# An out-projection in two halves of its rows, and a new order in a differential attention, in a two-block transformer kernel

## The reference

```python
h = rms_norm_2(x, mix_norm_g[layer])
proj = h @ w_in[layer]
da_q, da_k, da_v, sb_q, sb_k, sb_v, c_q, c_kv, k_r = jnp.split(proj, pts, axis=-1)
y_a = diff_attention(da_q, da_k, da_v, ...)        # 4 heads, columns 0 to 511 of y
y_b = stick_breaking(sb_q, sb_k, sb_v, ...)        # 4 heads, columns 512 to 767
y_c = latent_attention(c_q, c_kv, k_r, ...)        # 4 heads, columns 768 to 1023
x = x + jnp.concatenate([y_a, y_b, y_c], axis=-1) @ w_out[layer]
```

## Time and profile before

| | |
|---|---|
| median of three runs | 3553.13 us |
| the profiled execution | 3550.04 us |
| its span | 3548.2 us |
| TensorE matmuls, busy | 3166.5 us, 89% |
| VectorE, busy | 1626.1 us, 46% |
| ScalarE, busy | 1455.8 us, 41% |
| GpSimd, busy | 759.2 us, 21% |
| mean granted TensorE clock | 0.927 |

### The profile page before, as it was taken

One profiled execution on the slowest core, in us unless ns is written; L12 is line 12 of the kernel. 1 busy time (PEld: TensorE's weight loads), 2 busy tenths in 40 slices (PEclk: granted clock), 3 DMA queues, 4 the chain that ended last, 5 costly groups with the idle time before them and its releaser, 6 DMA issues.

```text
span 3548.2 us, 43654 instructions
## 1 busy us (share of the span) xinstructions
PE 3166.5 (89%) x13571; PEld 2479.1 (70%) x13571; DVE 1626.1 (46%) x2425; ACT 1455.8 (41%) x2128; POOL 759.2 (21%) x320
## 2 busy tenths in 40 slices
PE   7999999799997757999968978699998897879998
PEld 5788887588885545888746756488876664658887
DVE  4544544666565437565556344421125535351113
ACT  3333333433344545343344555432334455442323
POOL 1233232000002310000021212144432111214442
PEclk8999999899998878999978989799998898979999
DMA  8322222233331212333221211133332111213332
GB/s 201 96 86 78 66 86 60 76 96 96 94 90 42 74 45 83 93 93 95 65 78 36 55 48 42 30 95 93 92 88 85 48 53 33 60 29 93 94 94 77
DMA packets 486165, 269.41 MB, mean 76 GB/s; under 512 B 9418, under 2 KB 477458, under 8 KB 485620
## 3 DMA queue, kind: packets, MB, share of 16 engines
q1 hardware_dynamic: 479236, 255.85, 25.6%
q10 hardware_dynamic: 6768, 11.62, 1.0%
HBM read 264.12 MB, written 12.21 MB: 78 GB/s over the span
## 4 chain that ended last, share of the span: by engine, by line
issue 54%; PE 29%; POOL 11%; DVE 3%; ACT 2%; DMA 0%; SPq 0%; POOLq 0%; ACTq 0%; DVEq 0%
POOL s_w_lo L625 11%; PE acc L664 8%; PE acc L665 8%; PE acc L670 7%; PE acc L667 1%; PE wide L691 1%; PE misc L938 1%; PE misc L665 0%; PE misc L664 0%; PE misc L670 0%; PE wide L664 0%; DMA s_raw<-attn_w_qkv 0%; SPq L520 0%; DVE s_sc L2022 0%; POOLq L102 0%
## 5 line engine op out<-in xcount | busy, mean ns | idle before, releaser
L625 POOL TENSOR_TENSOR s_w_lo<-s_raw,s_w_hi 128x1024 fp32r<-128x1024 f32 x316 | 759.0, 2402 | 2760.3 <-ACT s_w_hi L1236 2755.2
L664 PE MATMUL acc<-s_h_hi,s_w_hi 128*128 128x512 f32 (+1 forms) x2128 | 873.5, 410 | 119.5 <-POOL s_w_lo L625 44.4
L665 PE MATMUL acc<-s_h_lo,s_w_hi 128*128 128x512 f32 (+1 forms) x2128 | 847.0, 398 | 0.0
L670 PE MATMUL acc<-s_h_hi,s_w_lo 128*128 128x512 f32 (+1 forms) x1862 | 741.3, 398 | 0.0
L664 PEld LDWEIGHTS acc<-s_h_hi,s_w_hi 128*128 128x128 f32 x2128 | 409.1, 192 | 238.2 <-issue 73.0
L1236 ACT ACTIVATE s_w_hi<-s_raw 128x1024 fp32r<-128x1024 f32 x388 | 411.7, 1061 | 387.1 <-DVE s_x L2527 210.9
L665 PEld LDWEIGHTS acc<-s_h_lo,s_w_hi 128*128 128x128 f32 x2128 | 410.5, 193 | 94.9 <-issue 7.1
L670 PEld LDWEIGHTS acc<-s_h_hi,s_w_lo 128*128 128x128 f32 x1862 | 358.6, 193 | 83.9
L664 PE MATMUL acc<-s_hid_hi,s_w_hi 128*128 128x512 f32 x752 | 297.4, 395 | 0.0
L665 PE MATMUL acc<-s_hid_lo,s_w_hi 128*128 128x512 f32 x752 | 297.3, 395 | 0.0
L670 PE MATMUL acc<-s_hid_hi,s_w_lo 128*128 128x512 f32 x658 | 260.0, 395 | 0.0
(11 more groups left out here) (395 smaller groups left out, 4875.3 us busy)
## 6 DMA issues: line engine op xcount, KB each, us to landing
s_raw<-w_ff SPq DMA_DIRECT2D x128, 512.0 KB, 4.0
s_raw<-ffn_w_up SPq DMA_DIRECT2D x96, 512.0 KB, 3.9
s_raw<-attn_w_qkv SPq DMA_DIRECT2D x72, 512.0 KB, 3.6
s_raw<-ffn_w_down SPq DMA_DIRECT2D x48, 512.0 KB, 3.9
s_raw<-w_in SPq DMA_DIRECT2D x44, 512.0 KB, 4.0
s_raw<-lru_w_in SPq DMA_DIRECT2D x16, 512.0 KB, 3.9
s_raw<-w_out SPq DMA_DIRECT2D x16, 512.0 KB, 4.0
s_raw<-attn_w_o SPq DMA_DIRECT2D x8, 512.0 KB, 4.1
```

The costliest lines, as they stand in the source:

```text
L625: pool.tensor_tensor(w_lo_of[w][:], raw_b[s][:], w_hi_of[w][:].bitcast(F32), ALU.subtract).then_inc(sems["unit_ready"], 1)
L664: mm(out, ahi, bhi, start=start, stop=False, **kw)
L665: mm(out, ahi, blo, start=False, stop=False, **kw)
L670: mm(out, alo, bhi, start=False, stop=stop, **kw)
```

## The change

The weights of `w_out` are loaded in another cut: four units of rows 0 to 511 x 256 columns, then four of rows 512 to 1023 x 256 columns. The first four chunks of y, which the differential attention makes, are split at the start of the latent attention into `early_hi` and `early_lo` (memory of the stick-breaking queries and keys, and two free chunks of `h_hi` and `h_lo`). The first half is multiplied inside the latent attention, as 8 tiles of 12 matmuls: tiles 0 to 3 into `misc`, two in the prologue and one in each of heads 0 and 1, tiles 4 to 7 into the two banks, around the softmax of head 3. VectorE adds each onto x. The second half stands where the out-projection stood, with 12 matmuls per tile; tiles 0 and 1 do chunks 4 to 6 before chunk 7 is there. ScalarE's splits of weights go with it: two before the four casts, two in head 2, two in head 3, four in `onto_residual`.

In the latent attention the sum of the query's squares comes before the rotation, and the key's sum goes to a bank of its own, so that ScalarE takes both Ln from different places; the casts of the key come first.

In the differential attention the scores of a head are issued between the chunks of the next query unit, the transposes of its weights before every second chunk of the next value unit, and the key's sum before chunk 3 of that unit, from a second buffer of squares. The sum over a head's output comes behind the value transpose, and its norm before the next head's scores on VectorE. The three units with which stick-breaking begins are issued under head 3, and the norm of that head's output inside `sb_heads`. In the diff some 8 or 12 columns of indentation are cut.

```diff
+early_hi = [t_[:] for t_ in (qh, ql, kh, kl)]
+early_lo = [t_[:, c, :] for t_ in (h_hi, h_lo) for c in (6, 7)]
 by_token = lambda ap: ap.rearrange("p k n -> p (k n)").rearrange("p (t c) -> p t c", t=TT)
...
-    for n in range(KC):
-        unit(wo2[:, :, n * P:(n + 1) * P])
+    for first in (0, KC // 2):
+        for n in range(KC // 2):
+            s = raw_b[count.slot()]
+            part_unit(s[:].rearrange("p k n -> p (k n)").rearrange("p (k n) -> p k n", k=KC // 2),
+                      wo2[:, first:first + KC // 2, n * 2 * P:(n + 1) * 2 * P])
...
+    next_unit = lambda before=None: unit_of(h_hi, h_lo, before=before)
+    def da_scores(k):
+        q, m = divmod(k, 2)
+        w = (q + 1) * P
+        o, r = next_wide(), slice(q * P, w)
+        three(o[:, 0:w], qh[half(m), r], ql[half(m), r], kh[half(m), 0:w], kl[half(m), 0:w],
+              True, True, "wide_full")
+    def da_turn(k):
+        q = k // 2
+        if k % 2 == 0:
+            pe.wait_ge(sems["p_ready"], count("p_ready"))
+            turn4(next_wide(), [sd[:, 0, TRI[q] + j * P:TRI[q] + (j + 1) * P] for j in range(q + 1)], "wide_full")
+    def da_keys_sum(k):
+        if k == 3:
+            head_sum(HALVES, first=1)
+    def da_turn_and_sum(k):
+        da_turn(k)
+        da_keys_sum(k)
+    next_unit(lambda k: pe.wait_ge(sems["h_lo"], count("h_lo")))
+    stats()
+    next_unit()
+    head_sum(HALVES)
+    next_unit(da_keys_sum)
+    turn_v()
     for h in range(HEADS_2):
-        unit_of(h_hi, h_lo, before=(lambda k: pe.wait_ge(sems["h_lo"], count("h_lo"))) if h == 0 else None)
-        if h == 0:
-            stats()
-        unit_of(h_hi, h_lo)
-        head_sum(HALVES)
-        if h:
-            turn_a()
-        unit_of(h_hi, h_lo)
-        head_sum(HALVES)
-        if h:
+        pe.wait_ge(sems["hn_lo"], count("hn_lo", 2))
+        next_unit(da_scores)
+        next_unit()
+        if h < HEADS_2 - 1:
+            head_sum(HALVES)
+            next_unit(da_turn_and_sum)
             weigh_values()
-        turn_v()
-        pe.wait_ge(sems["hn_lo"], count("hn_lo", 2))
-        for q in range(TT):
-            for m in range(2):
-                w = (q + 1) * P
-                o, r = next_wide(), slice(q * P, w)
-                three(o[:, 0:w], qh[half(m), r], ql[half(m), r], kh[half(m), 0:w], kl[half(m), 0:w],
-                      True, True, "wide_full")
-        if h:
+            turn_v()
             head_sum(ONES)
-    turn_a()
-    weigh_values()
-    head_sum(ONES)
+        else:
+            next_unit(da_turn)
+            weigh_values()
...
+        head_sum(ONES, MLA_W, squared="mla_sq")
+        pe.wait_ge(sems["mla_sq"], count("mla_sq"))
+        if past := count("acc_freed", lag=count.banks):
+            pe.wait_ge(sems["acc_freed"], past)
+        mm(bank[count.bank()][0:MLA_W, :], square[0:MLA_W, ONES, 0:MLA_W], sq[0:MLA_W, 1, :], start=True,
+           stop=True).then_inc(sems["acc_full"], 1)
+        count("acc_full")
+        count.outs += 1
...
+    count.units += 2
+    def out_chunks(o, n, chunks, hi, lo, start, stop):
+        w = lambda of, c: flat(of, count.slot())[:, (c % 4) * 2 * P + n % 2 * P:(c % 4) * 2 * P + n % 2 * P + P]
+        for c in chunks:
+            last = stop and c == chunks[-1]
+            mm(o, w(w_hi_b, c), hi[c], start=start and c == chunks[0], stop=False)
+            mm(o, w(w_hi_b, c), lo[c], start=False, stop=False)
+            if last:
+                mm(o, w(w_lo_b, c), hi[c], start=False, stop=True).then_inc(sems[stop], 1)
+                count(stop)
+            else:
+                mm(o, w(w_lo_b, c), hi[c], start=False, stop=False)
+    def early_tile(n, o, sem):
+        if n % 2 == 0:
+            pe.wait_ge(sems["unit_ready"], count("unit_ready"))
+        out_chunks(o, n, range(4), early_hi, early_lo, True, sem)
+        if n % 2:
+            count.units += 1
+    def early_in_misc(n):
+        take_misc("dve")
+        early_tile(n, misc[:], "wo_full")
+    def early_in_bank(n):
+        if past := count("acc_freed", lag=count.banks):
+            pe.wait_ge(sems["acc_freed"], past)
+        early_tile(n, bank[count.bank()][:], "acc_full")
+        count.outs += 1
     mla_values()
     mla_products(0)
+    pe.wait_ge(sems["o_lo"], count("o_lo", 4))
+    early_in_misc(0)
     head_sum(HALVES)
+    early_in_misc(1)
     head_sum(HALVES)
     take_misc("dve")
...
     mla_sums()
-    for h in range(HEADS_2):
-        if h < HEADS_2 - 1:
-            mla_products(h + 1)
+    for h in range(HEADS_2 - 1):
+        mla_products(h + 1)
         mla_scores(h)
         if h:
             mla_weigh(h - 1, TT)
-        if h < HEADS_2 - 1:
-            mla_sums()
+        if h < 2:
+            early_in_misc(2 + h)
+        mla_sums()
         if h == 2:
             head_sum(HALVES)
         mla_turn()
+    mla_scores(HEADS_2 - 1)
+    mla_weigh(HEADS_2 - 2, TT)
+    early_in_bank(4)
+    early_in_bank(5)
+    mla_turn()
+    early_in_bank(6)
     mla_weigh(HEADS_2 - 1, 0)
+    early_in_bank(7)
     head_sum(HALVES)
-    count.units += 2
+    late = ([ys_hi[:, c, :] for c in range(KC)], [ys_lo[:, c, :] for c in range(KC)])
     for n in range(KC):
-        unit_of(ys_hi, ys_lo, before=(lambda k: pe.wait_ge(sems["o_lo"], count("o_lo"))) if n == 0 else None)
+        if n % 2 == 0:
+            pe.wait_ge(sems["unit_ready"], count("unit_ready"))
+        if n == 0:
+            first = [bank[(count.outs + b) % count.banks] for b in range(2)]
+            for b in range(2):
+                pe.wait_ge(sems["acc_freed"], count("acc_freed", lag=count.banks))
+                for c in (4, 5, 6):
+                    if b == 0:
+                        pe.wait_ge(sems["o_lo"], count("o_lo"))
+                    out_chunks(first[b][:], b, [c], *late, c == 4, None)
+            pe.wait_ge(sems["o_lo"], count("o_lo"))
+        if n < 2:
+            out_chunks(first[n][:], n, [7], *late, False, "acc_full")
+        else:
+            if past := count("acc_freed", lag=count.banks):
+                pe.wait_ge(sems["acc_freed"], past)
+            out_chunks(bank[count.bank()][:], n, range(4, KC), *late, True, "acc_full")
+        count.outs += 1
+        if n % 2:
+            count.units += 1
...
+        head_square(tn[:, 1, :], part=1)
         head_rstd(SUB)
         head_hi(qh[:], tn[:, 0, :], SUB ** -0.5)
-        head_square(tn[:, 1, :])
...
+    for c in range(4):
+        fn(early_hi[c], yo[:, c, :], ACT.Copy).then_inc(sems["o_hi"], 1)
+        act.wait_ge(sems["o_hi"], count("o_hi"))
     norm_output(SUB)
     fn(sq[:, 0, :].rearrange("p (n k) -> p n k", n=2), tn[:, :, 0:N_MEM], ACT.Square).then_inc(sems["hn_sq"], 1)
...
     def mla_hi(h):
         head_rstd(MLA_W, MLA_W)
-        head_rstd(MLA_W, MLA_W, dst=sd[0:MLA_W, 1, S:2 * S])
+        rs_k = sd[0:MLA_W, 1, S:2 * S]
+        act.wait_ge(sems["acc_full"], count("acc_full"))
+        fn(rs_k, bank[count.bank()][0:MLA_W, :], ACT.Ln, bias=eps[0:MLA_W, 0:1], scale=1.0 / MLA_W).then_inc(sems["mla_ln"], 1)
+        count("acc_freed")
+        count.outs += 1
+        act.wait_ge(sems["mla_ln"], count("mla_ln"))
+        fn(rs_k, rs_k, ACT.Exp, scale=-0.5).then_inc(sems["hn_rstd"], 1)
+        act.wait_ge(sems["hn_rstd"], count("hn_rstd"))
+        freed()
...
+    nc.vector.memset(bd[0:CHUNK, :, S - CHUNK:S], NEG).then_inc(sems["bd_cut"], 1)
+    dve.wait_ge(sems["bd_cut"], count("bd_cut"))
+    for h in range(HEADS_2):
+        da_scores(h)
+        if h < HEADS_2 - 1:
+            o = output()
+            scaled(tn[:, 0, :], o[:])
+            da_weights()
+            o = output()
+            scaled(tn[:, 1, :], o[:])
+            da_queries()
+            turned_a()
+            da_keys()
+            values()
+            take_output()
+            turned_v()
+            da_output(h)
+        else:
+            sb_lo(0)
+            da_weights()
+            sb_lo(1)
+            turned_a()
+            values()
+            take_output()
...
         count("wide_freed")
+    for c in range(4):
+        dve.wait_ge(sems["o_hi"], count("o_hi"))
+        tt(early_lo[c], yo[:, c, :], early_hi[c].bitcast(F32), ALU.subtract).then_inc(sems["o_lo"], 1)
+        count("o_lo")
+    def early_from_misc(n):
+        dve.wait_ge(sems["wo_full"], count("wo_full"))
+        tt(x[:, n, :], x[:, n, :], misc[:], ALU.add).then_inc(sems["misc_dve"], 1)
+        count("misc_dve")
+    def early_from_bank(n):
+        o = output()
+        tt(x[:, n, :], x[:, n, :], o[:], ALU.add).then_inc(sems["acc_freed"], 1)
+        count("acc_freed")
+    early_from_misc(0)
     head_norm([(yo[:, 5, :], od[:], 0)], "sb_out_g_2")
+    early_from_misc(1)
     keys = tn[:, :, 0:N_MEM]
...
+        dve.wait_ge(sems["hn_rstd"], count("hn_rstd", 2))
+        output()
+        tt(kr[R, :], tn[R, 1, :], rs_k[R, :], ALU.mult).then_inc(sems["acc_freed"], 1)
+        dve.wait_ge(sems["acc_freed"], count("acc_freed"))
```

(28 more changed lines are left out.)

153 lines of the change are left out of this document (76 added, 77 removed).

## The result

| | median, us | runs | range |
|---|---|---|---|
| before | 3552.49 | 4 | 3548.35 to 3557.21 |
| changed | 3619.82 | 4 | 3618.24 to 3623.18 |

The ratio is 1.019, with a 95% interval from 1.0173 to 1.0208. Forecast was 3517, in a range up to 3543. The loss is 67 us, some 34 in each layer. The page of the changed kernel answers to the earlier trace rows: as many matmuls as before, and TensorE busy 93.5 us longer.

A forecast was written before the change was run, and what follows sets the result against it. The prediction took matmuls to bound the whole kernel, but VectorE-ScalarE-TensorE chains its attention stages. Differential -10.6 and latent -7.2 us per layer, twice, gave -35.6: 3514.4 from the profiled 3550.0, 3517 on the median's footing; 8-in-10 range 3485 to 3543.

The forecast's parts named there:

- 8 additions and 8 maxima, 3.9 + 3.9 less overlap: 15.6: Differential head: VectorE's additions and maxima on the scores end 15.6 us after the end of `s_kl`.
- 26.3 us of PE work: Differential head: unit matmuls, scores, sums, transposes and values total 26.3 us, under a chain of 34.5 us.
- First chain: Differential head 0: the key sum runs inside the value unit, so its chain ends earlier, -3.3 us per layer.
- Tail: Differential head 3 to first stick-breaking score: 32.8 us instead of 42.4, -9.6 per layer.
- Moved sum: One sum moves from the differential tail into the stick-breaking stage, where PE has no gap: +0.9 us per layer.
- Latent prologue: Latent attention up to its first scores: net +10 us per layer, bounds +4 and +13.
- late half: Second half of the out-projection: VectorE's work of 25.4 us in 22.4 of matmuls costs 0, at worst +4.
- The collisions: Differential weights: two GpSimd operations of 2.5 us fall on the four multiply-adds, 2.0 us more per head.
- rival 1: Collisions on the differential weights stay away and the latent prologue takes its low bound: 3473, half of it 3495; chance 0.15.
- The fifth: Differential scores wait for banks between chunks; short waits keep PE at 1.2 GHz: 3567 to 3628; chance 0.04.
- The third: PE stands in the middle of a differential unit, head period 37 or more: 3551; chance 0.06.
- the fourth: All three GpSimd splits of each differential head collide with VectorE, +2.1 us per head: 3534; chance 0.10.

The follow-up runs named there:

- warm: Changed kernel plus 16 or 17 discarded matmuls per differential head in the two waits ahead of the scores; 3551.40 us.
- scores_first: Changed kernel with the eight score tiles of a differential head ahead of the next query unit instead of between its chunks; 3549.39 us.
- tail_and_latent: Kernel before with the change's latent half, and the new differential order only behind the scores of head 3; 3523.62 us.
- tail_latent_busy: tail_and_latent plus 14 discarded matmuls per differential head, before the scores and ahead of the fifth tile; 3513.68 us.
- busy_everywhere: tail_latent_busy plus discarded 128x256 matmuls in the latent prologue, ahead of its third head's sum and in the memory attention; 3493.32 us.
- new_order_mended: Changed kernel with scores ahead of the unit, VectorE's weights ahead of the query's eviction, and 16 to 22 discarded matmuls per head; ratio 0.9925.

## Why the prediction was wrong

**The step that failed** is "8 additions and 8 maxima, 3.9 + 3.9 less overlap: 15.6". It took VectorE's own durations and did not ask when the tiles come. In the changed kernel each tile stands behind three unit matmuls. VectorE's and GpSimd's rows of that head:

```profile
1894.81 0.69 DVE L2370 TENSOR_REDUCE s_sm<-s_sd 128x1 f32<-128x512 f32 x1
1895.66 0.69 DVE L2325 TENSOR_TENSOR s_tn<-acc,s_rstd 128x512 f32<-128x512 f32 x1 [0.17 <-PE acc L673]
...
1897.95 2.53 DVE L2384 SCALAR_TENSOR_TENSOR s_sd<-s_sd,s_sm 128x256 f32<-128x256 f32 x1
1900.40 2.56 DVE L2382 TENSOR_SCALAR s_sd<-s_sd,s_sm 128x384 f32<-128x384 f32 x1
...
1897.67 2.53 POOL L631 TENSOR_TENSOR s_w_lo<-s_raw,s_w_hi 128x1024 fp32r<-128x1024 f32 x1 [26.76 <-ACT s_w_hi L1323]
```

From the end of `s_kl` (1867.96) the first addition begins after 8.3 us (forecast 8.1), the last maximum ends after 27.5 (15.6), the weights 9.3 behind it (8.9), the next `s_kl` 10.5 behind those (10.0): 47.4, against 34.5. So 11.9 of the 12.9 us of a head are this one term. The clock makes most of it, not all. In warm, at 2.4 GHz, the last maximum ends 17.9 us behind `s_kl`, still 2.3 more than forecast:

```profile
1895.41 0.69 DVE L2325 SCALAR_TENSOR_TENSOR s_kl<-s_tn,s_kh 128x512 fp32r<-128x512 f32 x1 [0.70 <-ACT s_kh L1632]
...
1913.30 0.69 DVE L2380 TENSOR_REDUCE s_sm<-s_sd 128x1 f32<-128x512 f32 x1
```

Behind it stands the second fault: the 26.3 us of PE work, which "the chain bounds", were counted at full clock and without changes of rows. TensorE is busy for 42.0 us in this head, and even in warm the eight tiles between the chunks take 5.3 us where 3.5 was counted.

**Step by step, in the first layer.** First chain -1.5 (forecast -3.3). Head 0 to 1: 47.6 (29.8). Heads 1 to 3: 47.4 and 47.2 (34.5 each). Tail: 39.6 (32.8), still 2.8 less than before. Moved sum: 1.7 longer in the stick-breaking stage (0.9). Latent prologue +8.5 (+10): the first early tile starts at 2129.33, 11.8 us behind the last stick-breaking matmul (12.1). Latent heads +3.0 (+1.4). Scores of head 3 to the last out-projection matmul: 44.5 (44.5); no cover was lost in the late half. The memory attention became 2.3 shorter, which I had not forecast and did not look into. Sum: +33.1, and 34.6 in the second layer.

**The collisions** came as counted: two on the weights of this head, 2.53 and 2.56 us where scores_first has 0.49 for the first, just before the operation of GpSimd, which there fell on the next one alone (2.62). The other was a one-input operation with per-partition scalars, which takes 0.41 us in the kernel before. So rival 1's "only DVE operations with two SBUF inputs are stretched" does not hold.

**The rivals.** The fifth had the mechanism, TensorE at 1.2 GHz, and its threshold (a period over 39) was passed. It had the wrong trigger: no wait stands between the chunks. It put all on a share of low-clock work in the whole head, where it is one stretch of 20 us that never recovers, and at 0.04 it was far too cheap: the half clock behind a wait and the 0.83 of the stage were read and not applied to the moved scores. Its "units that run dense recover within a unit" held for whole units and not for chunks between tiles. The third's threshold, 37, was passed too, by 37.6 in scores_first and warm. Its stop in the middle of a unit is there, ahead of the key's sum in the value unit, but it lasts 1.5 us in the changed kernel, 0.6 in scores_first and 3.1 in warm; how much of the period hangs on it no run shows. The third collision of the fourth did not come.

## What to carry to other kernels

Before matmuls of few rows are put between those of 128, count the changes: each costs 0.2 us at 2.4 GHz and 0.3 at 1.2 here, and where the halves stood side by side, that is lost too. A stretch of such single changes kept the clock with which it was entered in every run here, so look at what TensorE does just ahead of it. And when a chain is priced by the durations of one engine, ask for each step whether its input is there: a consumer of 16 quick operations is paced by the producer that was moved apart.

## What the runs showed that I had not expected

- TensorE, with no visible gap, stayed at a granted clock of 0.50 for 20.0 to 20.2 us in every head of the changed kernel (0.51 in one), and at 1.00 through the same instructions in warm.
- Matmuls with discarded results in its waits made a kernel faster. tail_and_latent took 3521.43 to 3527.78 in four runs and tail_latent_busy 3513.45 to 3515.02 beside it; the two layers went from 975.3 to 962.2, and to 942.5 in busy_everywhere.
- The clock can fall some 2 us behind a wait of under 1 us. In the third group of stick-breaking scores the same instructions ran with the same wait ahead (0.93 us) at a low clock in tail_and_latent and at full clock in tail_latent_busy (10 us windows, in that order), which makes most of the 3.6 us between these two up to the first latent score. new_order_mended shows both in one execution: the window with that group has 0.67 in the first layer and 1.00 in the second. The two windows:

```profile
2020.00:2030.00 10.00, 10.00 (x23) 6.20 (x23) 4.11 (x8) 8.47 (x17) 0.00 (x0) 0.52 0.00 1
```

```profile
2020.00:2030.00 10.00, 9.84 (x43) 7.26 (x42) 3.54 (x7) 8.07 (x16) 0.00 (x0) 1.00 0.01 2
```

What decides between them is open. Open too is why the layers began up to 9 us later or 0.3 earlier than before in the profiles, in code that no kernel changed; all stage lengths here are taken within a layer.
